# Hybrid decoder trunk on one Trainium2 core: when turned rows are copied out, when returned rows are combined, and the order of the end

## The reference

```python
logits = (h @ router).astype(F32)
topv, topi = lax.top_k(logits, TOP_K)          # TOP_K = 2 of 8 experts
wts = jax.nn.softmax(topv, axis=-1)
...
for e in range(N_EXPERTS):
    out = out + gates[..., e:e + 1] * swiglu(h, w1[e], w3[e], w2[e])
x = x + gt2 * out                              # then: y = rmsnorm(x, final_g)
```

## Time and profile before

| | us |
|---|---|
| median of 3 runs | 1497.73 (1490.84 to 1502.0) |
| the profiled execution | 1499.95 |
| its span, first to last instruction | 1498.2 |
| PE busy | 1421.7 (95% of the span) |
| DVE busy | 1039.7 (69%) |
| ACT busy | 826.9 (55%) |
| POOL busy | 57.7 (4%) |
| mean granted clock | 0.962 |
| `y_rows_hbm<-x_rows`, the zero store, 6656 KB, issue to landing | 25.9 |

### The profile page before, as it was taken

One profiled execution on the slowest core, in us unless ns is written; L12 is line 12 of the kernel. 1 busy time (PEld: TensorE's weight loads), 2 busy tenths in 40 slices (PEclk: granted clock), 3 DMA queues, 4 the chain that ended last, 5 costly groups with the idle time before them and its releaser, 6 DMA issues.

```text
span 1498.2 us, 20931 instructions
## 1 busy us (share of the span) xinstructions
PE 1421.7 (95%) x8031; PEld 1197.3 (80%) x8031; DVE 1039.7 (69%) x1227; ACT 826.9 (55%) x862; POOL 57.7 (4%) x72
## 2 busy tenths in 40 slices
PE   8999999999999999998789999999999999999866
PEld 4888878999978887886568888888888888888655
DVE  3488434455435764378558888888888888888777
ACT  3343434444333426245447777777777777777635
POOL 1000000000000000021000000000000001000000
PEclk8899999999999999979889999999999999999979
DMA  9986686854569722938649999999999999999960
GB/s 301 308 278 199 218 262 197 266 187 159 190 195 329 229 91 78 401 115 318 222 145 384 396 355 396 374 375 396 353 395 374 373 395 356 394 386 375 398 222 29
DMA packets 264137, 427.41 MB, mean 285 GB/s; under 512 B 10353, under 2 KB 152377, under 8 KB 264066
## 3 DMA queue, kind: packets, MB, share of 16 engines
q1 hardware_dynamic: 243712, 397.22, 75.5%
q10 hardware_dynamic: 17938, 20.70, 4.0%
q0 software_dynamic: 2416, 8.52, 1.5%
HBM read 408.93 MB, written 17.55 MB: 285 GB/s over the span
## 4 chain that ended last, share of the span: by engine, by line
PE 84%; DVE 8%; ACT 4%; issue 2%; DMA 1%; ACTq 0%; POOL 0%; DVEq 0%
PE ps L902 20%; PE ps L904 19%; PE ps L903 19%; PE ps L789 7%; PE ps L890 4%; PE ps L673 2%; DVE slab_lo L1929 2%; PE ps L741 2%; ACT slab_hi L1450 1%; PE ps L1058 1%; PE ps L950 1%; DVE uT L1678 1%; DMA y_rows_back<-y_rows_hbm,lot_indices 1%; PE ps L768 1%; PE ps L627 1%
## 5 line engine op out<-in xcount | busy, mean ns | idle before, releaser
L1929 DVE TENSOR_TENSOR slab_lo<-ring,slab_hi 128x2048 fp32r<-128x2048 f32 x264 | 605.0, 2296 | 112.1 <-ACT slab_hi L1450 109.8
L1450 ACT CAST slab_hi<-ring 128x2048 fp32r<-128x2048 f32 x261 | 497.1, 1907 | 134.9 <-PE ps L904 134.6
L902 PE MATMUL ps<-slab_hi,tokens_hi 128*128 128x512 f32 (+1 forms) x768 | 296.3, 386 | 27.8 <-DVE slab_lo L1929 26.3
L904 PE MATMUL ps<-slab_hi,tokens_lo 128*128 128x512 f32 (+1 forms) x768 | 291.0, 379 | 0.0
L903 PE MATMUL ps<-slab_lo,tokens_hi 128*128 128x512 f32 (+1 forms) x768 | 289.9, 377 | 0.0
L902 PEld LDWEIGHTS ps<-slab_hi,tokens_hi 128*128 128x128 f32 x768 | 146.9, 191 | 56.9 <-DVE slab_lo L1929 30.4
L904 PEld LDWEIGHTS ps<-slab_hi,tokens_lo 128*128 128x128 f32 x768 | 146.9, 191 | 27.9
L903 PEld LDWEIGHTS ps<-slab_lo,tokens_hi 128*128 128x128 f32 x768 | 147.4, 192 | 26.1
L789 PE MATMUL ps<-hT,ring 128*128 128x264 f32 x704 | 161.0, 387 | 0.0
L902 PE MATMUL ps<-slab_hi,act_hi 128*128 128x512 f32 x352 | 142.8, 406 | 13.2 <-DVE slab_lo L1929 13.2
L789 PEld LDWEIGHTS ps<-hT,ring 128*128 128x128 f32 x704 | 132.3, 190 | 22.3 <-issue 0.8
(11 more groups left out here) (405 smaller groups left out, 1749.4 us busy)
## 6 DMA issues: line engine op xcount, KB each, us to landing
ring<-in_moe_w SPq DMA_DIRECT2D x264, 1024.0 KB, 13.1
ring<-in_mod_w SPq DMA_DIRECT2D x48, 1024.0 KB, 8.6
ring<-in_ffn_w SPq DMA_DIRECT2D x30, 1024.0 KB, 5.7
ring<-in_w_in SPq DMA_DIRECT2D x24, 1024.0 KB, 10.1
ring<-in_w_out SPq DMA_DIRECT2D x8, 1024.0 KB, 6.4
y_rows_hbm<-x_rows ACTq DMA_DIRECT2D x1, 6656.0 KB, 25.9
out_new_S_sample<-S ACTq DMA_DIRECT2D x8, 512.0 KB, 2.9
y_rows_hbm<-y_rows ACTq DMA_DIRECT2D x7, 512.0 KB, 6.3
```

The source lines that it names most:

```text
L902: mm(out, x, w, start=start, stop=False)
L904: return mm(out, xl, w, start=False, stop=stop)
L1450: cp(wH[t % 3][:, :], w).then_inc(s_hi, 1)
L1929: tt(wL[t % 3][:, :], w, wH[t % 3][:, :].bitcast(fp32), ALU.subtract).then_inc(s_lo, 1)
```

## The change

Five edits. (1) In the first lot `rows_out(n)` stands behind ACT's cast of slab t = 14 + 2n in place of 12 + 2n, and the gate rows' store one slab later; two of DVE's table steps move one slab later (9 to 10, 11 to 12). (2) The combining steps of the last lot stand at t = 12, 13, 14, then 18, 19, 20, then 24, 25, 26, and `placed` at t = 16. (3) The zero rows come from a tile of their own (`zero_rows`, 128 x 512), which POOL clears when layer 0's projections are done. ACT stores it in the dense feed-forward part, at slab d = 15, and only to the six blocks of `y_hbm` from lot 7 on. (4) The tiles of the end go in the order 2, 0, 1 (`FINAL_ORDER`); DVE's small half-mean steps (L2119) stand between the additions of the second half. (5) At the end DVE scales both halves of tile 0 and the second of tile 1, POOL and ACT the first half of tile 1 and all of tile 2.

```diff
--- before.py
+++ after.py
@@ -129,6 +129,7 @@
...
         own_lot = nc.alloc_sbuf_tensor_at("own_lot", [P, 3, 2, MAXLOTS], fp32, offset=short + 4 * 4096)
+        zero_rows = nc.alloc_sbuf_tensor_at("zero_rows", [P, 512], fp32, offset=mixed + 4 * (4 * SLAB + KC * N))
         h2raw = nc.alloc_sbuf_tensor_at("h2_rows_sum", [P, 3, D], fp32, offset=u_at)
...
@@ -509,7 +510,7 @@
...
             sp.dma_start(o["y_prompt"][0, 0:P, :], xr[:, 0, :]).then_inc(s_out, 16)
-            sp.wait_ge(s_frv, 4)
+            sp.wait_ge(s_fr, 2)
             sp.dma_start(o["y_sample"].rearrange("b t c -> (b t) c"), x8[0:NS, :]).then_inc(s_out, 16)
...
@@ -542,8 +543,9 @@
...
 
+            pool.wait_ge(used, FFN)
+            g.memset(zero_rows[:, :], 0.0).then_inc(s_h2z, 1)
             pool.wait_ge(s_y, L)
-            g.memset(xr[:, 0, :], 0.0).then_inc(s_h2z, 1)
             g.memset(h2H[:, 2, :].bitcast(fp32), 0.0).then_inc(s_h2z, 1)
...
@@ -604,10 +606,11 @@
...
             pool.wait_ge(s_gld, 48)
-            for q in range(2):
-                qs = slice(q * 512, (q + 1) * 512)
-                pool.wait_ge(s_sq, KC * 2 * L + 3 * q + 2)
-                g.tensor_tensor(out=xr[:, 1, qs], in0=xr[:, 1, qs], in1=fg_row[:, qs], op=ALU.mult).then_inc(s_xg, 1)
+            pool.wait_ge(s_sq, KC * 2 * L + 3)
+            g.tensor_tensor(out=xr[:, 1, 0:512], in0=xr[:, 1, 0:512], in1=fg_row[:, 0:512], op=ALU.mult)\
+                .then_inc(s_xg, 1)
+            pool.wait_ge(s_sq, KC * 2 * L + 4)
+            g.tensor_tensor(out=x8[0:NS, :], in0=x8[0:NS, :], in1=fg_row[0:NS, :], op=ALU.mult).then_inc(s_xg, 1)
 
...
@@ -1092,11 +1095,11 @@
...
                     qs = slice(q * 512, (q + 1) * 512)
-                    for t in range(3):
-                        if t == 0:
+                    for t in FINAL_ORDER:
+                        if t == FINAL_ORDER[0]:
                             pe.wait_ge(s_yt, final_lot * 2 + q + 1)
                         mm(ps[FINAL_BANK[t][q]][:, :], placed[:, t * P:(t + 1) * P], yH[:, qs], start=True, stop=False)
-                        if t == 0:
+                        if t == FINAL_ORDER[0]:
                             pe.wait_ge(s_yl, q + 1)
...
@@ -1313,9 +1316,6 @@
...
                     vector_stores(l)
-                    act_.wait_ge(s_h2z, 1)
-                    act_.dma_start(y_hbm.rearrange("(n p) d -> p n d", p=P),
-                                   xr[:, 0, :].unsqueeze(1).broadcast_to([P, MAXLOTS + 1, D])).then_inc(s_yst, 16)
                 if l == 0:
...
@@ -1379,6 +1379,11 @@
...
                     vector_stores(0)
+                if d == 15:
+                    act_.wait_ge(s_h2z, 1)
+                    act_.dma_start(y_hbm[(NE - 1) * LOT:, :].rearrange("(p r) (h d) -> p (r h) d", p=P, h=2),
+                                   zero_rows[:, :].unsqueeze(1).broadcast_to([P, 2 * (MAXLOTS + 2 - NE), 512]))\
+                        .then_inc(s_yst, 16)
                 if d % 2 == 0 and d <= 2 * G:
...
@@ -1393,6 +1398,8 @@
...
                     q = (d - 2 * G - 5) // 3
+                    if q == 0:
+                        act_.wait_ge(s_yst, 16)
                     for c in (2 * q, 2 * q + 1):
...
@@ -1452,12 +1459,11 @@
...
                         store_outputs(i, constant)
-                    if first and t - 1 in ROWS_AT:
-                        if ROWS_AT[t - 1] == 0:
+                    if first and t - 3 in ROWS_AT:
+                        if ROWS_AT[t - 3] == 0:
                             act_.wait_ge(s_hst, 32)
-                            act_.wait_ge(s_yst, 16)
-                        rows_out(ROWS_AT[t - 1])
-                    if first and t - 3 in ROWS_AT and ROWS_AT[t - 3] == 7:
+                        rows_out(ROWS_AT[t - 3])
+                    if first and t - 4 in ROWS_AT and ROWS_AT[t - 4] == 7:
                         act_.wait_ge(s_xtr, 8)
...
@@ -1496,26 +1502,27 @@
...
             def final_square(q, t):
-                act_.wait_ge(s_x, 3 * q + t + 1)
+                act_.wait_ge(s_x, 3 * q + FINAL_ORDER.index(t) + 1)
                 rows = (xr[:, 0], xr[:, 1], x8[0:NS])[t]
...
 
-            for t in range(3):
+            for t in FINAL_ORDER:
                 final_square(0, t)
-            for t in range(3):
+            for n, t in enumerate(FINAL_ORDER):
                 final_square(1, t)
                 r = rs_row[0:ROWS[t], t:t + 1]
-                act_.wait_ge(s_feb, t + 1)
-                act_.wait_ge(s_sq, KC * 2 * L + 4 + t)
+                act_.wait_ge(s_feb, n + 1)
+                act_.wait_ge(s_sq, KC * 2 * L + 4 + n)
                 ch(A(r, sq_part[0:ROWS[t], 2 * t + 1:2 * t + 2], ACT.Ln, scale=1.0 / D, bias=sq_eps[0:ROWS[t], t:t + 1]))
...
             act_.wait_ge(s_rs, 3 * L + 3)
-            for q in range(2):
-                act_.wait_ge(s_xg, q + 1)
-                A(xr[:, 1, q * 512:(q + 1) * 512], xr[:, 1, q * 512:(q + 1) * 512], ACT.Copy, scale=rs_row[:, 1:2])\
-                    .then_inc(s_fr, 1)
-            act_.wait_ge(s_fr, 2)
+            act_.wait_ge(s_xg, 1)
+            A(xr[:, 1, 0:512], xr[:, 1, 0:512], ACT.Copy, scale=rs_row[:, 1:2]).then_inc(s_fr, 1)
+            act_.wait_ge(s_xg, 2)
+            A(x8[0:NS, :], x8[0:NS, :], ACT.Copy, scale=rs_row[0:NS, 2:3]).then_inc(s_fr, 1)
+            act_.wait_ge(s_fr, 1)
+            act_.wait_ge(s_frv, 3)
             act_.dma_start(o["y_prompt"][0, P:T, :], xr[:, 1, :]).then_inc(s_out, 16)
...
@@ -2109,22 +2116,19 @@
...
                 qs = slice(q * 512, (q + 1) * 512)
-                for t in range(3):
-                    dve.wait_ge(s_fp, 3 * q + t + 1)
+                for n, t in enumerate(FINAL_ORDER):
+                    dve.wait_ge(s_fp, 3 * q + n + 1)
                     tt(out_rows[t][:, qs], out_rows[t][:, qs], ps[FINAL_BANK[t][q]][0:ROWS[t], :], ALU.add)\
                         .then_inc(s_x, 1)
-                if q == 0:
-                    for t in range(3):
-                        dve.wait_ge(s_sq, KC * 2 * L + t + 1)
+                    if q:
+                        dve.wait_ge(s_sq, KC * 2 * L + n + 1)
                         ts(sq_eps[0:ROWS[t], t:t + 1], sq_part[0:ROWS[t], 2 * t:2 * t + 1], 1.0 / D, EPS,
                            ALU.mult, ALU.add).then_inc(s_feb, 1)
-            for t in (0, 2):
-                dve.wait_ge(s_rs, 3 * L + t + 1)
-                dve.wait_ge(s_x, 4 + t)
-                for q in range(2):
-                    qs = slice(q * 512, (q + 1) * 512)
-                    stt(out_rows[t][:, qs], out_rows[t][:, qs], rs_row[0:ROWS[t], t:t + 1], fg_row[0:ROWS[t], qs],
-                        ALU.mult, ALU.mult).then_inc(s_frv, 1)
+            for t, q in ((0, 0), (0, 1), (1, 1)):
+                dve.wait_ge(s_rs, 3 * L + 2 + t)
+                qs = slice(q * 512, (q + 1) * 512)
+                stt(out_rows[t][:, qs], out_rows[t][:, qs], rs_row[:, t:t + 1], fg_row[:, qs], ALU.mult, ALU.mult)\
+                    .then_inc(s_frv, 1)
 
...
@@ -2227,11 +2231,12 @@
...
 TURN_AT = dict(FORM_AT)
-TABLE_AT = {3: 0, 5: 1, 9: 2, 11: 3, 13: 4, 15: 5, 17: 6, 19: 7}
+TABLE_AT = {3: 0, 5: 1, 10: 2, 12: 3, 13: 4, 15: 5, 17: 6, 19: 7}
 TABLE_TURN = 7
 ROWS_AT = {11 + 2 * n: n for n in range(8)}
-COMBINE_AT = {14 + k: k for k in range(9)}
-PLACE_AT = 24
+COMBINE_AT = {12 + 6 * t + k: 3 * t + k for t in range(3) for k in range(3)}
+PLACE_AT = 16
+FINAL_ORDER = (2, 0, 1)
 FINAL_BANK = ((0, 1), (2, 3), (6, 7))
...
```

## The result

| | before | after |
|---|---|---|
| median, us | 1497.37 (4 runs, 1490.84 to 1502.0) | 1452.99 (4 runs, 1445.74 to 1455.55) |
| the profiled execution | 1499.95 | 1450.97 |
| its span | 1498.2 | 1449.2 |
| PE busy | 1421.7 | 1400.0 |
| mean granted clock | 0.962 | 0.981 |

The ratio is 0.970, with an interval of 0.965 to 0.975. The profiled executions lie 49.0 us apart, and 48.7 was the sum.

What follows compares the result with a forecast made beforehand. PE was taken as the bound, weight transfers close behind, held up in the first and last lots. Gains 31.6 + 16.8 + 0 + 0.3 = 48.7 us gave 1451.3 profiled, 1449.0 on the median; forecast 1450, range 1439 to 1466.

Steps and rivals of the forecast that it cites:

- undisturbed round of 6.1 us: First lot: two slabs (5.5 us) and four transposes (0.60); each of 8 rounds falls to this from 10.05.
- 3 us to spare between copy and next turn: First lot: copy ready 2.5 us after slab 11 + 2n, PE's next turn at 5.5, so no new wait.
- late pairs by the table steps: First lot: slab pairs where DVE's table steps need up to 7.1 us against 6.1; some tenths lost, 1 us each at worst.
- 12 us for the clock: First lot: 24 of 80 us at 1.2 GHz, half of which is lost.
- what remains: Last lot: loss left after moving the combining steps, 4.6 us, taken off 21.4 to give a gain of 16.8.
- the gathers: Last lot, tile 1: DVE still waits 0.7 to 2.0 us, its lead takes 1.2, leaving 0.5 on PE.
- DVE's own work in the groups: Last lot: three steps add 3.9 us, less 1.4 spare and 1.2 lead; 1.3 on PE per tile, `placed` 0.2 more.
- the prediction's other reckoning: End: POOL's longer product slows two of three DVE scalings by 1.05 us each; no gain or 1 us lost.
- The gathers' rival: Last lot: a tile's gathers take over some 14 us from third step to landing, PE waits; 1460 us, chance 0.08.
- PE waiting for the copies: First lot: PE's next turn waits for the later copy, rounds keep about half of 3.95 us; 1466 us, chance 0.04.
- the clock staying low: First lot: transposes every 6 us keep the clock low, 12 us not regained; 1462 us, chance 0.02.
- the weights as the bound: Expert lots: without PE's pauses each slab waits for its weight transfer, 0.24 us longer; 1513 us, chance 0.03.

Runs made afterwards that it cites:

- copies_by_two: The kernel before with only the copies of the turned rows moved, two slabs behind instead of three; one run, 1465.55 us.
- combine_only: The kernel before with only the combining steps and `placed` moved as in the change; ratio to before 0.986 (0.978 to 0.994).
- spread_steps: The changed kernel with combining steps at 11, 12, 14, 19, 21, 24, 29, 31, 32, placed at 7, prompt's end stores halved; 1448.26 us, 0.968 of before.
- zero_end_only: The changed kernel with the moves of copies and combining steps undone, leaving zero rows and end; ratio to before 0.998 (0.995 to 1.002).

## Why the prediction was right, point by point

**Edit 1.** 31.6 us forecast, 31.9 measured in two kernels. The undisturbed round of 6.1 us is 6.0; no wait came in its place, and the 3 us to spare between copy and next turn are borne out by copies_by_two, which gave some of them up for nothing. The late pairs by the table steps cost nothing either: PE has no wait for DVE there. The 12 us for the clock were a little low: they come from a window that holds seven of the eight low stretches, and all eight make 13.7. This share was not a term of the sum, which took the whole rounds.

**Edit 2.** 16.8 forecast, 14.6 measured. The step that was mis-sized is what remains: 4.6 us forecast, 6.9 measured (97.7 less 90.8). The starts of DVE's subtractions of the slabs 12, 18, 24 and 30 show where it lies. In the last lot:

```profile
1363.44 2.29 DVE L1936 TENSOR_TENSOR slab_lo<-ring,slab_hi 128x2048 fp32r<-128x2048 f32 x1 [0.78 <-ACT slab_hi L1457]
...
1382.28 2.28 DVE L1936 TENSOR_TENSOR slab_lo<-ring,slab_hi 128x2048 fp32r<-128x2048 f32 x1
...
1402.21 2.29 DVE L1936 TENSOR_TENSOR slab_lo<-ring,slab_hi 128x2048 fp32r<-128x2048 f32 x1 [0.38 <-ACT slab_hi L1457]
...
1421.89 2.29 DVE L1936 TENSOR_TENSOR slab_lo<-ring,slab_hi 128x2048 fp32r<-128x2048 f32 x1 [0.38 <-ACT slab_hi L1457]
```

The three groups take 18.8, 19.9 and 19.7 us. In the lot before it in the same trace the four starts are 1267.56, 1284.49, 1301.43 and 1318.35, 16.9 us apart. So the group that waits for no gather costs 1.9 us, `placed` with it, where the sum had 1.3 and 0.2, and the two others cost 3.0 and 2.8, 1.1 and 0.9 more. Of these 7.7 us 0.6 are caught up behind slab 30 (5.8 us to slab 32, where the lot before takes 6.4) and 0.1 ahead of slab 12. Two terms are off.

The first is the gathers: 0.5 us in the sum, 2.0 in the trace. The 1.1 and 0.9 have the size of DVE's waits of 1.13 and 0.91, so these reached PE in full: PE's first waits behind them are 1.42 and 1.10 us (at 1389.39 and 1409.10), and behind the first step of the group without a gather there is none. The forecast had a wait of 0.7 to 2.0, so its size was right, but let DVE's lead of 1.2 take it. The same lead was counted again for the three steps of each group: it can be spent once. And the waits are what the gathers' longer time leaves. I took 12.3 us from the third step to the next tile's first for tile 1, and of the tile of 8 rows I said that it "needs no longer than this". The rows give 12.9 for tile 1 (1372.75 to 1385.69) and 12.6 for the tile of 8 rows (1392.80 to 1405.41), where it had been 10.2 (1432.31 to 1442.49). POOL's issues of the gathers in the changed kernel, for the earlier trace rows, say why:

```profile
1374.24 2.75 POOL L605 DMA_INDIRECT y_rows_back<-y_rows_hbm,lot_indices  x1 [22.82 <-DVE x_rows L2066]
1377.29 2.50 POOL L605 DMA_INDIRECT y_rows_back<-y_rows_hbm,lot_indices  x1 [0.30 <-issue]
1394.32 2.67 POOL L605 DMA_INDIRECT y_rows_back<-y_rows_hbm,lot_indices  x1 [14.54 <-DVE x_rows L2066]
1397.30 2.45 POOL L605 DMA_INDIRECT y_rows_back<-y_rows_hbm,lot_indices  x1 [0.30 <-issue]
```

The second issue of a pair takes 2.50 and 2.45 us, against 0.94 before, when DVE had stopped 0.5 us earlier and stood waiting for this very gather. The first of each pair took 2.7 us in both kernels and began while DVE was subtracting a slab. In combine_only the second issues take 2.49 and 2.44. So the gathers' time was measured in a state that the change takes away: an issue that begins in a gap of DVE. The 1.6 us more of the second issue don't come back in full for tile 1: from its end to DVE's step it took 6.8 us before and 5.9 after. For the tile of 8 rows it was 4.8 and 5.7. What made this part shorter and longer was not tried apart. The sum had one tile waiting, and there were two.

The second is DVE's own work in the groups, 1.9 us in the group that shows it alone, where 1.3 and 0.2 were in the sum. spread_steps, in which no gather is waited for and the steps stand apart, has 1.9 left of 6.9 for all nine steps, so gathers and crowding together were 5.0: by the groups some 2.0 for the gathers, which leaves 3.0 for the crowding; the two were not tried apart.

**Edit 3.** 0 forecast. Removing the old store and adding the new one in the dense stage shows in no stretch (zero_end_only); the new store took 18.0 us to land where 12 were estimated, beside the weight loads (share 0.99 and 0.97 meanwhile), and PE waited for nothing.

**Edits 4 and 5.** 0.3 forecast, 0.0 between the two profiled executions. The end of the changed kernel, DVE, SP's queue and ACT's:

```profile
1441.56 3.09 DVE L2130 SCALAR_TENSOR_TENSOR x_rows<-x_rows,lot_tables,final_gain_row 128x512 f32<-128x512 f32 x3 [1.32 <-ACT lot_tables L1518]
...
1444.02 0.38 SPq L512 DMA_DIRECT2D out_y_prompt<-x_rows  x1
...
1444.74 0.34 ACTq L1526 DMA_DIRECT2D out_y_prompt<-x_rows  x1
```

Counted from the gating (1433.62 after, 1482.59 before), the last issue comes at 11.1 us instead of 11.5: the 0.3 are there. (In the kernel before it is SP's small store at 1494.11, not ACT's at 1494.05, which the prediction took.) But the first of the two large stores comes at 10.4 instead of 10.1, so the two are 0.7 us apart instead of 1.3, and the last instruction is at 15.6 in both. spread_steps, whose stores begin by halves, ends 1.1 us sooner. This fits an end that is set by the stores' transfer and not by their issue; whether the halves or the earlier start did it was not separated. Over all profiles the old order gave 15.5 to 16.4 and the new one 15.5 to 15.6, so a few tenths may be the new order's. One of the three scalings again took long, 1.77 us against 0.74 for the two others: the 1.05 us of the earlier trace rows were paid once, and not twice as in the prediction's other reckoning.

**The rivals.** The gathers' rival didn't come: 12.9 and 12.6 us stay below its 14, though both gathers are waited for. PE waiting for the copies, the clock staying low, and the weights as the bound didn't come: the window of the first lot has a clock of 1.00 with a turn every 6 us, and no cast waits for the ring. The chances were right on the side where the time fell.

## What to carry to other kernels

An engine that feeds another may wait for it without cost, as long as the wait is shorter than its lead; count the lead in slabs before placing a chore, and spend it once. Here one slab more of distance was enough, a wait of 1.3 us in each round remained, and the third slab gained nothing. Where the fed engine is TensorE, a wait costs more than its length: 2 us of waiting in each round of 6 cost 4. And a latency that was measured while its user stood still is too short: the engine that will now be at work can slow the one that issues the transfer.

## What the runs showed of the hardware that was not expected

- POOL's issue of an indirect DMA took 1.85 to 2.85 us where it began while DVE was at the subtraction of a slab (128 x 2048, both inputs in SBUF), and 0.86 to 1.07 where it began in a gap of DVE; this holds for every such issue in the nine profiles. Beside the short subtraction of the tokens (0.68 us, one input in PSUM), begun 0.5 us before, it took 0.98 to 1.03. Before, the second of the pairs for the tiles 1 and 2 began in gaps (0.94 and 0.86), after, beside a subtraction (2.50 and 2.45). The gather for lot 1 has both in one place of the program: 2.84 us at 694.15 beside a subtraction in the kernel before, 1.05 at 694.50 in a gap in the changed one. No run changed this alone.
- The time to slab 3 of the first lot differs by 11 us (664.7 to 675.7) between executions whose instructions are the same up to there, along with the mean granted clock of that stretch (0.97 to 0.94). Without combine_only it is still 7 us, 664.7 to 671.8, at 0.97 and 0.95. The undisturbed stretches, by the starts of one group of instructions, repeat to 0.2 us in all nine profiles (slab 3 to 11 of the first lot 29.1 to 29.3, lots 1 to 6 567.0), and tell effects of 2 us apart that the whole times don't.
- Four fillings of eight matmuls removed six of eight low stretches of the clock and made the stretch 9.1 us shorter. Two of the six were in rounds that had not been filled.
